# Expert weight tiles of a hybrid decoder step: another order of slot reuse, and room for two more tiles ahead

## What is computed

```python
p_g = softmax(t @ wg + bg);  g_sel = argmax(p_g)            # one of 4 groups
e_sel = (t @ we + be) of that group                         # 4 experts in it
top_p, top_i = top_k(softmax(e_sel), 2)
gate = weights of the two experts, times p_g[g_sel]         # (tokens, 16)
a = t @ w_gate[e];  u = t @ w_up[e]                         # each 2048 x 512
act = silu(a) * u * gate[e]
out = sum over e of act @ w_down[e]                         # 512 x 2048
x = x + out
```

## Time and profile before

| | |
|---|---|
| median of 3 runs | 1513.38 us (1507.8 to 1514.45) |
| the profiled execution's own time | 1512.04 us |
| its span, first to last instruction | 1510.3 us |
| PE, DVE, ACT, POOL busy | 94%, 38%, 12%, 53% of the span |
| moved by DMA | 377 MB, 250 GB/s over the span |
| mean granted TensorE clock | 0.987 of full speed |

### The profile page before, as it was taken

The page is one execution under the profiler, slowest core; times in us unless marked ns, Lnnn a source line. Parts: engine busy times, 40 slices in busy tenths (PEclk is TensorE's granted clock), DMA queues, the critical chain, the costliest instruction groups (busy, mean ns, idle before and its releaser), DMA issues. The chain is left out here.

```text
span 1510.3 us, 25557 instructions
## 1 busy us (share of the span) xinstructions
PE 1426.8 (94%) x9308; PEld 1095.4 (73%) x9308; DVE 568.0 (38%) x1074; ACT 186.9 (12%) x383; POOL 795.8 (53%) x1453
## 2 busy tenths in 40 slices
PE   6999999999989999999999989979998998998997
PEld 6999999998879999987777689963344343443444
DVE  3646578739573533213111443151122121121224
ACT  5001321000000010013222100051000000000002
POOL 3877587879967767743545357511451350431500
PEclk9999999999999999999999989989999999999999
DMA  8444244445544444563888624757999999999991
GB/s 251 140 143 161 89 137 147 159 157 185 175 158 167 140 166 141 188 231 137 323 331 312 211 84 149 276 217 301 420 422 422 421 422 421 422 421 422 422 422 70
DMA packets 106120, 377.07 MB, mean 250 GB/s; under 512 B 12421, under 2 KB 12421, under 8 KB 76290
## 3 DMA queue, kind: packets, MB, share of 16 engines
q1 hardware_dynamic: 103778, 371.68, 64.8%
q10 hardware_dynamic: 2272, 4.42, 0.9%
HBM read 369.30 MB, written 6.77 MB: 249 GB/s over the span
## 5 line engine op out<-in xcount | busy, mean ns | idle before, releaser
L837 PE MATMUL ps<-hT,tiles 128*128 128x144 f32 x1792 | 294.5, 287 | 8.8 <-ACT kv_stage L1418 3.2
L746 POOL COPY A<-A 128x16 f32 x952 | 146.2, 217 | 289.5 <-issue 289.4
L837 PE MATMUL ps<-A,tiles 128*128 128x144 f32 x1792 | 265.1, 288 | 6.2 <-DVE mT L1661 3.9
L837 PEld LDWEIGHTS ps<-hT,tiles 128*128 128x128 f32 x1792 | 250.7, 191 | 10.7 <-ACT kv_stage L1418 3.5
L837 PEld LDWEIGHTS ps<-A,tiles 128*128 128x128 f32 x1792 | 239.9, 192 | 7.4 <-issue 4.8
L701 POOL TENSOR_TENSOR tiles<-tiles 128x512 f32<-128x512 f32 x88 | 116.8, 1327 | 190.6 <-DMA tiles<-in_w_in 69.7
L837 PE MATMUL ps<-tiles 128*128 128x144 f32 x960 | 170.7, 287 | 0.0
L1173 PE MATMUL ps<-tiles,A 128*64 128x512 f32 x512 | 148.0, 602 | 15.7 <-DMA tiles<-in_expert_w_up 9.6
L837 PEld LDWEIGHTS ps<-tiles 128*128 128x128 f32 x960 | 140.0, 191 | 0.0
L894 PE MATMUL ps<-tiles,mT 128*128 128x256 f32 x512 | 132.8, 382 | 4.1 <-ACT kv_stage L1418 4.1
L1680 DVE COPY pair_sums<-ps 128x144 f32<-128x144 f32 x44 | 13.5, 307 | 306.7 <-PE ps L837 306.6
(11 more groups left out here) (347 smaller groups left out, 1702.0 us busy)
## 6 DMA issues: line engine op xcount, KB each, us to landing
tiles<-in_expert_w_down SPq DMA_DIRECT2D x56, 1024.0 KB, 23.4
tiles<-in_w_in SPq DMA_DIRECT2D x40, 1024.0 KB, 5.1
tiles<-in_expert_w_gate SPq DMA_DIRECT2D x32, 1024.0 KB, 17.5
tiles<-in_expert_w_up SPq DMA_DIRECT2D x32, 1024.0 KB, 17.9
A<-in_expert_w_up SPq DMA_DIRECT2D x24, 1024.0 KB, 24.6
tiles<-in_xa_w_k SPq DMA_DIRECT2D x16, 1024.0 KB, 5.1
tiles<-in_w_out SPq DMA_DIRECT2D x16, 1024.0 KB, 5.1
tiles<-in_xa_w_q SPq DMA_DIRECT2D x16, 1024.0 KB, 5.1
```

The source lines that it names most:

```text
L746: m = nc.gpsimd.tensor_copy(xe[:, :, at + n:at + n + 1], h_moe_or_zero[:, :, bass.ds(token, 1)])
L837: return mm(one(u + mp, x, TH), w[:, kp, mp, :], rhs, start=(first and g == 0 and kp == 0), stop=(g == 3 and kp == 1), skip_group_check=True)
```

## The change

It lays `wr` and `before` into mT, `before_rep`, `place_iota` and `token_no` into the end of `tiles`, `pick` into the end of hT, and `spread` into `rstd`. What this frees in A becomes a fourth part of `more_slots`, at the place of the old `pick` and `spread`; it is slot 14. The slots are used in turn: tile m of a group has slot m modulo 15, so tiles 0 to 14 have slots 0 to 14 and tiles 15 to 23 slots 0 to 8. The lag becomes 9 for tiles 0 to 8 of a group (from the second group on), 24 for 9 to 14, and 15 for 15 to 23. Tile 14 of the first group waits, like 12 and 13, for `h_tok_rest`. Tile 15 of the first group alone goes into `y_pair`, after the event `h_moe_rest` (TensorE's turn back of the second chunk), and signals slot 0's semaphore, after tile 0 has landed. So both branches of the first pair (16 tiles) are issued ahead of the wait for the job list, and SyncE's loop body begins with the down tiles.

```diff
-PE_EVENTS, MOE_SLOTS = 11, 14
+PE_EVENTS, MOE_SLOTS = 11, 15
...
-        pick, at = cut(at, 3, 2 * C)
-        spread, at = cut(at, T)
-        more_slots, at = cut(at, 3, KT * TW)
-        wr, at = cut(at, DB, 32)
-        before, at = cut(at, P)
-        before_rep, at = cut(at, P)
-        place_iota, at = cut(at, 2, C)
-        token_no, at = cut(at, 4)
+        more_slots, at = cut(at, 4, KT * TW)
...
+        spare_mT = mT[:, :, :].rearrange("p a b -> p (a b)")
+        wr = spare_mT[:, 3456:3456 + DB * 32].rearrange("p (b n) -> p b n", b=DB)
+        before = spare_mT[:, 3456 + DB * 32:]
+        before_rep, place_iota, token_no = tiles[:, 17408:17536], tiles[:, 17536:17664], tiles[:, 17664:17668]
+        pick = hT[:, :, :].rearrange("p b n -> p (b n)")[:, 2 * KT * TW:2 * KT * TW + 6 * C].rearrange("p (c n) -> p c n", c=3)
+        spread = rstd_flat[:, 0:T]
...
-        moe_slots = [ring[:, 7, :]] + [more_slots[:, n, :] for n in range(3)]
+        moe_slots = [ring[:, 7, :]] + [more_slots[:, n, :] for n in range(1, 4)]
...
+        moe_slots += [more_slots[:, 0, :], y_pair]
...
         def moe_slot(m):
-            m %= 24
-            return m if m in (12, 13) else m % 12
+            return m % 24 % MOE_SLOTS
         def moe_lag(m):
-            return 24 if m % 12 < 2 else 12
-        def moe_tile(m):
-            return moe_slots[moe_slot(m)]
+            j = m % 24
+            return 24 - MOE_SLOTS if j < 24 - MOE_SLOTS else 24 if j < MOE_SLOTS else MOE_SLOTS
+        def moe_tile(m, i):
+            return moe_slots[MOE_SLOTS if i is None and m == MOE_SLOTS else moe_slot(m)]
         def wait_moe_tile(pe, m, i=None):
-            pe.wait_ge(moe_loaded[moe_slot(m)], plus(16 * (m // moe_lag(m) + 1), i, 16 * 24 // moe_lag(m)))
+            shared = moe_slot(m) < 24 - MOE_SLOTS
+            n = 2 * (m // 24) + 1 + (m % 24 >= MOE_SLOTS) if shared else m // 24 + 1
+            pe.wait_ge(moe_loaded[moe_slot(m)], plus(16 * n, i, 32 if shared else 16))
...
             def moe_load(m, src, i=None):
-                if m >= MOE_SLOTS:
+                if i is None and m == MOE_SLOTS:
+                    after_event(sp, EVENT["h_moe_rest"])
+                    sp.wait_ge(moe_loaded[moe_slot(m)], 16)
+                elif m >= MOE_SLOTS:
                     sp.wait_ge(tile_used, plus(TILE["moe"] + m - moe_lag(m) + 1, i, 24))
                 elif m >= 12:
                     after_event(sp, EVENT["h_tok_rest"] + 1)
...
-                sp.dma_start(moe_tile(m), src).then_inc(moe_loaded[moe_slot(m)], 16)
+                sp.dma_start(moe_tile(m, i), src).then_inc(moe_loaded[moe_slot(m)], 16)
...
             branch_tiles(0, 0, range(8))
-            branch_tiles(1, 8, range(MOE_SLOTS - 8))
+            branch_tiles(1, 8, range(8))
             sp.wait_ge(jobs_ready, 2)
...
             with sp.Fori(0, n_loops) as i:
                 experts = [expert(i * 2 + n) for n in range(4)]
-                branch_tiles(experts[1], 8, range(MOE_SLOTS - 8, 8), i)
                 down_tiles([experts[0], expert(i * 2 + 1)], 16, i)
                 branch_tiles(experts[2], 24, range(8), i)
-                branch_tiles(experts[3], 32, range(MOE_SLOTS - 8), i)
+                branch_tiles(experts[3], 32, range(8), i)
             experts = [expert(n_loops * 2 + n) for n in range(2)]
-            branch_tiles(experts[1], 8, range(MOE_SLOTS - 8, 8), n_loops)
             down_tiles([experts[0], expert(n_loops * 2 + 1)], 16, n_loops)
```

More of the change, by code:

```diff
@@ L262, in build @@
         spare = mT[:, :, :].rearrange("p a b -> p (a b)")[:, 0:D]
+        spare_mT = mT[:, :, :].rearrange("p a b -> p (a b)")
         stat_sum = pair_sums[:, :, :].rearrange("p j n -> p (j n)")
+        wr = spare_mT[:, 3456:3456 + DB * 32].rearrange("p (b n) -> p b n", b=DB)
+        before = spare_mT[:, 3456 + DB * 32:]
+        before_rep, place_iota, token_no = tiles[:, 17408:17536], tiles[:, 17536:17664], tiles[:, 17664:17668]
+        place_iota = place_iota.rearrange("p (a n) -> p a n", a=2)
+        pick = hT[:, :, :].rearrange("p b n -> p (b n)")[:, 2 * KT * TW:2 * KT * TW + 6 * C].rearrange("p (c n) -> p c n", c=3)
+        spread = rstd_flat[:, 0:T]
         slot_token = tiles[0:1, SLOTS * KT * TW:SLOTS * KT * TW + 4 * C].bitcast(I32)
         y_nat = ring[:, 0:3, :]
-        moe_slots = [ring[:, 7, :]] + [more_slots[:, n, :] for n in range(3)]
+        moe_slots = [ring[:, 7, :]] + [more_slots[:, n, :] for n in range(1, 4)]
         moe_slots.append(kv_stage[:, :, :, :].rearrange("p a b c -> p (a b c)"))
@@ L1173, in branch @@
                             m = mm(ps[C * n:C * n + C, BRANCH_BANK + s, :], xe[:, b, C * s:C * s + C],
-                                   moe_tile(t + 2 * g + n).rearrange("p (k n) -> p k n", k=KT)[:, k, :],
+                                   moe_tile(t + 2 * g + n, i).rearrange("p (k n) -> p k n", k=KT)[:, k, :],
                                    start=(b == 0), stop=(b == DB - 1))
@@ L1236, in down @@
                             m = mm(ps[C * s:C * s + C, b, :], actT[:, s, k, :],
-                                   moe_tile(16 + 2 * k + s)[:, b * TW:(b + 1) * TW], start=(k == 0), stop=(k == KT - 1))
+                                   moe_tile(16 + 2 * k + s, i)[:, b * TW:(b + 1) * TW], start=(k == 0), stop=(k == KT - 1))
                     m.then_inc(tile_used, 2)
```

## The result

The changed kernel takes 1517.06 us (median of 20 runs, 1513.64 to 1521.3), the kernel before 1511.87 (20 runs, 1507.78 to 1515.89): ratio **1.0036**, 95% interval 1.0027 to 1.0046, or +5.2 us by the medians. The profiled execution took 1517.77 us with a span of 1516.1, 5.8 above that of before; the mean granted TensorE clock was 0.987 in both. One execution in all that follows, one of the twelve of order14, took 1874.59 us at a granted clock of 0.775 where the others had 0.98 to 0.99, and it is left out of that kernel's ratio.

The account below looks back on a forecast made before the run. The DMA stream of expert tiles, 2.485 us a tile, was taken as the bound. Profiled 1512.04 us plus 4.6 (tile 25 31.95 later, less 27.3 for 11 fewer tiles; scratch and later loops 0) gave 1516.6 us, range 1508 to 1524.

Parts of the forecast that it names:

- Two tiles ahead, -5.0 us of stream: Before the first branch: tiles 14 and 15 go into an empty DMA stretch, alone removing 5.0 us; added SyncE wait free.
- The order of reuse, tile 25 as the pivot: First group: tile 25 waits for tile 16, issued 31.95 us later with 11 tiles fewer behind (27.3): +4.6 us.
- the other end, by landings: Same delay of the stream counted by tile 25's landing, 1062.4 before and 1065.9 after: +3.5 us.
- The two holes: First group: DMA idle while tiles 24 and 25 wait for tiles 15 and 16, 1047.8 to 1053.7 and 1056.2 to 1062.4.
- Later loops, slack 1.9 us: Each later loop: tile 25 lands 22.96 us after tile 15, wanted at 24.85; slack 1.9 us, so no loss.
- Scratch, 0: Moved scratch tensors and 15th slot: same instructions on other addresses, below 1 us either way, taken as 0.
- First stall of PE near 1094 to 1101: Sign in PE's timeline: first stall on an up tile near 1094 to 1101 us instead of 1137.
- Tile 16 near 1025: Sign in SyncE's queue: tile 16, waiting for tiles 0 and 1 to be used, issued near 1025 us.
- The rival that the gain stays: DMA queue rides over tiles 24 and 25; stream ends two tiles earlier, 1507.1 us; chance 0.07.
- The one of a loss in every loop: Tile 25's slack fails in every loop: 1523.6 us at 1 us short a loop, 1530.6 at 2; chance 0.13.
- The one of no effect: Idle time falls where PE is the bound and PE's 5 us a loop of reserve swallows it: 1512 us; chance 0.08.

Follow-up runs that it names:

- order14: Kernel before with only the change's order of slot reuse (14 slots, old scratch, no output-buffer place): ratio to before 1.0017, stage +1.7 us.
- no_place: Changed kernel without tile 15's place in the output buffer; tile 15 waits for tile 0 and takes slot 0: ratio to before 1.0029, stage 440.4 us.
- lag12: Changed kernel's scratch, 15 slots and place, but slots paired as before (lags 12 and 24): ratio to before 0.9996, stage -1.3 us.
- hold_24: Changed kernel, but tiles 24 to 32 of every group wait for the tile 8 before instead of 9: ratio to before 1.0065, stage +8.1 us.
- mirrored: Changed kernel's slots and place, short lag 9 moved to tile 39 and down tiles, first down tiles issued ahead of SyncE's loop: ratio to before 0.9941.
- scratch_only: Kernel before with only the change's scratch places; 14 slots, order and waits as before: ratio to before 1.0002, stage 436.3 us.
- mirrored14: As mirrored, but with lags of 14 and 10 instead of 15 and 9: ratio to before 0.9949, stage 428.4 us.

## Why the prediction was right

The forecast was 1516.6 us; 1517.06 was measured. That the two are within 0.5 us is partly luck: the 20 runs spread over 7.7 us, the stage came out 0.3 below the forecast of +4.6, and the medians moved 0.9 more than the stage. The range, 1508 to 1524, would have held no effect as well, so it is the holes and the stage that speak for the mechanism. By its steps:

- *Two tiles ahead, -5.0 us of stream.* They were issued at 1006.36 and 1012.00 into an empty stretch (DMA share 1.01 and 1.00 from 1008 to 1016), and the added wait cost nothing: SyncE's wait for the job list shrank from 18.8 us to 11.0. no_place shows that one of them is worth 0.2 us, not 2.5, as the prediction said of both: the idle time eats them.
- *The order of reuse, tile 25 as the pivot.* Written +4.6 with a lower end of +3.5; the stage says +4.3. The same formula gave 2.1 for order14 (1.7 measured), -1.5 for lag12 (-1.3) and 7.1 for hold_24's first loop (8.1 less six times 0.28 is 6.4). It is 0.2 to 0.7 us too large in size each time; the other end, by landings, was 0.8 too small. A lone tile landed after 4.7 us (tile 24) and 5.0 us (tile 25) here, and not 5.1. For mirrored the same way of counting was 3.5 us off, because it left a place out.
- *The two holes.* Forecast 1047.8 to 1053.7 and 1056.2 to 1062.4, 12.1 us. Seen: low rates from 1048 to 1064, with the 1.5 us of the later start in them, and 11.5 us lost.
- *Later loops, slack 1.9 us.* Tile 25's fellow of the next group went 17.63 us after tile 15's landing (1120.44 - 1102.81), so the slack was 2.1 by the 5.1 us of the earlier trace rows. With the tile before it still on its way (to 1125.2) this tile took 7.2 us and landed after 24.83 us, at its time in the stream (24.85). hold_24 took the slack away, and the dips came.
- *Scratch, 0.* scratch_only: 0.0 in the stage.
- *First stall of PE near 1094 to 1101.* It first stood ahead of 1082.60, for 0.36 us: tile 31, forecast for 1081.0, came just after PE wanted it. The first stall over 1 us ended at 1097.51, at tile 37, forecast for 1095.9. Both lie within 0.1 us once the 1.5 us of the later start are taken off.
- *Tile 16 near 1025.* It went at 1027.59. The late start of branch 0 explains 1.5 us. The other 1 us lies in SyncE and not in the use of tile 0: it went 7.3 us after the start of branch 0, but 6.2 in mirrored, which waits for the same use and issues it ahead of the loop. It stands ahead of a hole, which would take up such a delay.

That the medians moved by 5.2 us and the stage by 4.3 is within the interval of the ratio (4.1 to 7.0 us), and says nothing of a further cost.

The rival that the gain stays fell with no_place and the hole. (The argument against it, "falls short by 4 us even if PE were a pair faster", counts wrong: 1051.9 - 1047.8 = 4.1 is without the faster pair.) The one of a loss in every loop fell for the changed kernel; hold_24, which takes tile 24's wait one pair further, shows such a loss beginning, 0.28 us a loop, and no run shows where between the two it sets in. The one of no effect fell with the stream's end, which moved: the stretch 1475 to 1480 still has a DMA share of 0.79, where before had 0.00.

## What to carry to other kernels

Where a stream of transfers is the bound, count slots by the *shortest* distance between a tile and the one whose place it takes, at the moment when the consumer is furthest behind, and not by their number: issue is in order, so a single short distance holds up all behind it. The mirrored orders have distances of 9 and 10 too, but for the down tiles, where they made no hole; the one 9 that mirrored put where PE was still behind, at tile 39, made one. With 24 tiles on 15 slots the sum of the two distances of a shared slot is fixed, and the long one belongs where the consumer pauses. A tile fetched ahead was a gain where no hole came after it (1.7 of 2.5 us in the stage of mirrored14); ahead of a hole it only lengthened the hole (0.2 us in the changed kernel).

## What was not expected of the hardware

With an almost empty queue the DMA can move less than its busy share says. In mirrored, 1092 to 1096 us, the 16 engines were busy 0.99 of the time and moved 352 GB/s, in mirrored14, 1060 to 1064, 0.98 and 348, where the full stream has 1.01 and 422. The changed kernel shows where in a transfer this lies: tile 24, issued alone at 1053.35,

```profile
1054.00:1055.00 1.00, 0.35 (x4) 0.34 (x4) 0.61 (x1) 0.26 (x1) 0.00 (x0) 1.00 0.75 131
1055.00:1056.00 1.00, 0.76 (x7) 0.62 (x6) 0.20 (x1) 0.19 (x2) 0.20 (x2) 1.00 0.93 360
1056.00:1057.00 1.00, 0.44 (x2) 0.30 (x4) 0.23 (x1) 0.52 (x2) 1.00 (x9) 0.53 0.97 410
```

has its engines busy 0.75 of the first microsecond with 131 GB/s, and 0.97 of the third with 410. The same in mirrored14: 0.99 busy with 172 GB/s from 1063 to 1064, when tile 30, issued at 1062.00, comes in. So a stream whose tiles come just in time by the count of 2.485 us a tile already loses some tenths of a microsecond. Where every tile that waits was counted, the tile-by-tile count was good to 0.7 us in the stage. What the engines do in that first microsecond was not tried.
